# Normalising after the product in the second and third attention of a two-block layer stack

## What is computed

```python
# first block (called nsa): 4 groups x 4 heads, three softmaxes with gates
o = g[0] * o_cmp + g[1] * o_slc + g[2] * o_win
# second block, first layer (called ev): window over the tokens, plus context, plus a sink
p = jax.nn.softmax(jnp.concatenate([s_loc, s_ctx, s_sink], axis=-1), axis=-1)
o = jnp.einsum('bnkgqs,bnskd->bnqkgd', p[..., :nloc], vb) + jnp.einsum('bnkgqc,bckd->bnqkgd', p[..., nloc:nloc + lc], v_ctx)
# second block, second layer (called od): neighbourhood over the tokens, plus context
p = jax.nn.softmax(jnp.concatenate([s_loc, s_ctx], axis=-1), axis=-1)
```

## Time and profile before

| what | value |
|---|---|
| median of 3 runs | 2406.17 us (2405.99 to 2408.24) |
| the profiled execution | 2403.84 us |
| its span, first to last instruction | 2402.0 us |
| PE busy | 2318.0 us, 97% of the span |
| DVE, ACT, POOL busy | 1480.0, 921.2 and 249.1 us |
| mean granted TensorE clock | 0.982 of full speed |
| scores to last product of nsa | about 370 to 450 us of the span |
| the same of ev | about 1196 to 1263 us |
| the same of od | about 2130 to 2178 us |

### The profile page before, as it was taken

The page is one execution under the profiler, slowest core; times in us unless marked ns, Lnnn a source line. Parts: engine busy times, 40 slices in busy tenths (PEclk is TensorE's granted clock), DMA queues, the critical chain, the costliest instruction groups (busy, mean ns, idle before and its releaser), DMA issues.

```text
span 2402.0 us, 33724 instructions
## 1 busy us (share of the span) xinstructions
PE 2318.0 (97%) x14400; PEld 2015.2 (84%) x14400; DVE 1480.0 (62%) x1930; ACT 921.2 (38%) x1351; POOL 249.1 (10%) x235
## 2 busy tenths in 40 slices
PE   8999998889999999999989999999999999998999
PEld 7999895779998888888858888888888888878999
DVE  6584447577768776756765876424754333865544
ACT  6653336444454222224453322223422222544442
POOL 0030000101111101010010101100000101201110
PEclk9899998899999999999999999999999999999999
DMA  6444371255643544532202455222544322522553
GB/s 226 175 167 162 115 242 62 97 202 197 257 170 131 210 177 174 210 123 106 97 14 105 146 205 201 93 84 97 211 164 187 140 97 87 168 71 74 192 192 106
DMA packets 34834, 356.23 MB, mean 148 GB/s; under 512 B 3981, under 2 KB 6188, under 8 KB 8444
## 3 DMA queue, kind: packets, MB, share of 16 engines
q1 hardware_dynamic: 31788, 343.61, 38.6%
q0 software_dynamic: 2896, 10.46, 1.6%
HBM read 351.08 MB, written 1.13 MB: 147 GB/s over the span
## 4 chain that ended last, share of the span: by engine, by line
PE 89%; DVE 7%; ACT 3%; issue 1%; DMA 0%; POOL 0%; POOLq 0%; SPq 0%; DVEq 0%; ACTq 0%
PE psum L834 26%; PE psum L835 26%; PE psum L836 25%; PE psum L1126 2%; PE psum L882 1%; PE psum L883 1%; PE psum L884 1%; DVE ring_r L1825 1%; PE psum L1151 1%; DVE rr L1835 1%; PE psum L1121 1%; PE psum L1184 1%; PE psum L1095 1%; PE psum L1032 1%; PE psum L1023 1%
## 5 line engine op out<-in xcount | busy, mean ns | idle before, releaser
L834 PE MATMUL psum<-arena_r 128*128 128x256 f32 (+1 forms) x3384 | 1128.8, 334 | 20.5 <-DVE zT_r L1865 8.3
L836 PE MATMUL psum<-arena_r,ring_r 128*128 128x256 f32 (+1 forms) x3384 | 1119.3, 331 | 0.0
L835 PE MATMUL psum<-zT_r,arena_r 128*128 128x256 f32 (+1 forms) x2656 | 861.7, 324 | 0.0
L1351 ACT ACTIVATE arena_r<-ring 128x2048 fp32r<-128x2048 f32 (+1 forms) x252 | 473.5, 1880 | 705.8 <-PE psum L836 685.4
L834 PEld LDWEIGHTS psum<-arena_r 128*128 128x128 f32 x3384 | 637.2, 188 | 95.1 <-issue 21.8
L836 PEld LDWEIGHTS psum<-arena_r,ring_r 128*128 128x128 f32 x3384 | 639.3, 189 | 68.3
L1825 DVE TENSOR_TENSOR ring_r<-ring,arena_r 128x2048 fp32r<-128x2048 f32 (+1 forms) x252 | 568.3, 2257 | 195.5 <-ACT arena_r L1351 194.8
L835 PEld LDWEIGHTS psum<-zT_r,arena_r 128*128 128x128 f32 x2656 | 503.7, 190 | 45.1
L835 PE MATMUL psum<-arena_r 128*128 128x256 f32 (+1 forms) x1304 | 423.5, 325 | 0.0
L1976 DVE CUSTOM_DVE_ANT_0 psum<-arena,cb 128x1024 f32<-128x1024 f32 x256 | 318.1, 1302 | 0.0
L835 PEld LDWEIGHTS psum<-arena_r 128*128 128x128 f32 x1304 | 245.9, 189 | 20.4
(11 more groups left out here) (282 smaller groups left out, 1990.5 us busy)
## 6 DMA issues: line engine op xcount, KB each, us to landing
ring<-in_wf SPq DMA_DIRECT2D x75, 2048.0 KB, 7.9
ring<-in_w SPq DMA_DIRECT2D x41, 2048.0 KB, 7.9
arena<-in_w SPq DMA_DIRECT2D x72, 1024.0 KB, 9.8
ring<-in_wf SPq DMA_DIRECT2D x10, 1536.0 KB, 6.6
ring<-in_w SPq DMA_DIRECT2D x5, 1024.0 KB, 5.4
arena<-strip_scratch POOLq DMA_DIRECT2D x1, 2048.0 KB, 9.5
arena<-rpb_scratch POOLq DMA_DIRECT2D x16, 128.0 KB, 11.1
xT<-in_x SPq DMA_DIRECT2D x1, 1024.0 KB, 6.0
```

Of the source, the lines that this page charges most:

```text
L834: mm(b[c][:, at], whc, xh[:, k, at], start=(k == ks[0]), stop=False)
L835: mm(b[c][:, at], whc, xl[:, k, at], start=False, stop=False)
L836: last = mm(b[c][:, at], wlc, xh[:, k, at], start=False, stop=(k == ks[-1]))
L1351: A(W_hi[h % NHI][:, 0:n], ring[:, half_slot(h)], ACT.Identity).then_inc(sig("w_hi"), 1)
```

## The change

For ev and od, `turn` transposes the exponentials as they are, so that it no longer needs the diagonal matrices; it waits for all four exponentials of its unit instead. The diagonal matrices are still written by DVE (into two buffers in turn, the second one is `rr`), and a new step of PE, `spread_sums`, ahead of the last `multiply`, multiplies a block of ones by each of them: four matmuls of 128 rows by 64 by 128, which put the reciprocals of the sums on the rows and columns of the result's layout, in PSUM bank 4. ACT copies these 128 by 256 numbers to SBUF (into a half of `rt`) behind the last copy of the unit, and `att_done` multiplies the result by them in place of copying it. In DVE's loop `att_done(u-1)` now comes first, then `att_max(u+1, 1)`, then `att_norm(u)`, then `att_max(u+2, 0)`. For the first unit of an attention `att_max(u+1, 0)` and `att_max(u+1, 1)` come ahead of `att_norm(u)`. In nsa nothing changes.

```diff
--- before.py
+++ after.py
@@ -426,6 +426,14 @@
             at = (4 if g < 2 else 7) * BANK + (g % 2) * S
             return psum[:, at:at + S]
 
+        def att_sums(u):
+            return rt[:, S * (u % 2):S * (u % 2) + S]
+
+        def att_diag(u):
+            if u % 2:
+                return rr[:, :].rearrange("p (r t) -> p r t", r=4)
+            return E_diag if UNITS[u][0] == "ev" else O_diag
+
         def own(u, a, b):
             return small[:, 48 * (u % 2) + a:48 * (u % 2) + b]
 
@@ -1107,8 +1115,10 @@
                 def turn(i):
                     seg, blk = bs[i]
                     gb = gb0 + i
-                    if blk == bs[0][1]:
+                    if kind == "nsa" and blk == bs[0][1]:
                         pe.wait_ge(sig("att_p"), scaled_before(u) + seg + 1)
+                    if kind != "nsa" and i == 0:
+                        pe.wait_ge(sig("att_exp"), 4 * (u + 1))
                     if gb >= 2:
                         pe.wait_ge(sig("att_copied"), gb - 1)
                     pt = psum[:, (5 + gb % 2) * BANK:(6 + gb % 2) * BANK]
@@ -1117,13 +1127,8 @@
                             at = 2048 + (2 * (r % 2) + r // 2) * CMP_N if seg == 2 else place(seg, r) * S + blk * P
                         else:
                             at = r * BANK + blk * P
-                        if kind == "nsa":
-                            last = nc.tensor.transpose(pt[0:keys(i), r * P:(r + 1) * P], Pb[:, at:at + keys(i)],
-                                                       C("ident"))
-                        else:
-
-                            diag = (E_diag if kind == "ev" else O_diag)[:, r, :]
-                            last = mm(pt[:, r * P:(r + 1) * P], Pb[:, at:at + P], diag, start=True, stop=True)
+                        last = nc.tensor.transpose(pt[0:keys(i), r * P:(r + 1) * P], Pb[:, at:at + keys(i)],
+                                                   C("ident"))
                     last.then_inc(sig("att_turned"), 1)
 
                 def multiply(i):
@@ -1152,12 +1157,24 @@
                                       start=(i == 0), stop=(i == len(bs) - 1), skip_group_check=True)
                     last.then_inc(sig("att_mult"), 1)
 
+                def spread_sums():
+                    pe.wait_ge(sig("att_p"), scaled_before(u) + 1)
+                    diag = att_diag(u)
+                    for j in range(2):
+                        for a in range(2):
+                            at = 4 * BANK + j * P
+                            last = mm(psum[64 * a:64 * a + 64, at:at + P], C("ones")[:, 0:HD], diag[:, 2 * j + a, :],
+                                      start=True, stop=True)
+                    last.then_inc(sig("att_spread"), 1)
+
                 for i in range(len(bs)):
                     turn(i)
                     if i == min(2, len(bs) - 1):
                         between()
                     if i >= 1:
                         multiply(i - 1)
+                if kind != "nsa":
+                    spread_sums()
                 multiply(len(bs) - 1)
 
             def attention(u0, u1, Pb, PT, ready, beside=None, free_banks=None):
@@ -1675,6 +1692,9 @@
                         for part in range(4):
                             if parts_behind[part] == i and u + 1 < u1:
                                 att_exp(u + 1, Pb, part)
+                    if UNITS[u][0] != "nsa":
+                        act.wait_ge(sig("att_spread"), u - NSA_U[1] + 1)
+                        A(att_sums(u), psum[:, 4 * BANK:4 * BANK + S], ACT.Identity).then_inc(sig("att_spread_in"), 1)
 
 
             for i in range(2):
@@ -2371,14 +2391,8 @@
                 if kind == "ev":
                     link(v.tensor_tensor(out=sm[:, 0:4], in0=sm[:, 0:4], in1=own(u, 32, 36), op=ALU.add))
                 link(v.reciprocal(small[:, 36:40], sm[:, 0:4]))
-                first = (EV_U if kind == "ev" else OD_U)[0]
-                if u > first:
-                    dve.wait_ge(sig("att_turned"), batches_before(u))
-
-                v.tensor_tensor(out=E_diag if kind == "ev" else O_diag, in0=b3(C("ident"), 4, P),
+                v.tensor_tensor(out=att_diag(u), in0=b3(C("ident"), 4, P),
                                 in1=rep(small[:, 36:40], P), op=ALU.mult).then_inc(sig("att_p"), 1)
-                if u > first:
-                    att_done(u - 1, y)
 
             def att_done(u, y):
                 kind, g, t = UNITS[u]
@@ -2387,9 +2401,14 @@
                     k = 4 + 2 * g
                 else:
                     k = 2 * g
-                v.tensor_copy(y[:, k:k + 2, t * P:(t + 1) * P],
-                              psum[:, 7 * BANK:7 * BANK + 2 * P].rearrange("p (j t) -> p j t", j=2))\
-                    .then_inc(sig("att_out"), 1)
+                out, o = y[:, k:k + 2, t * P:(t + 1) * P], psum[:, 7 * BANK:7 * BANK + 2 * P]
+                o = o.rearrange("p (j t) -> p j t", j=2)
+                if kind == "nsa":
+                    v.tensor_copy(out, o).then_inc(sig("att_out"), 1)
+                else:
+                    dve.wait_ge(sig("att_spread_in"), u - NSA_U[1] + 1)
+                    v.tensor_tensor(out=out, in0=o, in1=att_sums(u).rearrange("p (j t) -> p j t", j=2), op=ALU.mult)\
+                        .then_inc(sig("att_out"), 1)
 
             def attention(u0, u1, Pb, y, beside=None, behind=None):
                 att_max(u0, (0, 1))
@@ -2398,11 +2417,17 @@
                 else:
                     att_max(u0 + 1, (0,))
                 for u in range(u0, u1):
-                    att_norm(u, Pb, y)
+                    kind = UNITS[u][0]
+                    if kind == "nsa":
+                        att_norm(u, Pb, y)
+                    elif u > u0:
+                        att_done(u - 1, y)
                     if u == u0 and beside is not None:
                         att_max(u0 + 1, (0,))
                     if u + 1 < u1:
                         att_max(u + 1, (1,))
+                    if kind != "nsa":
+                        att_norm(u, Pb, y)
                     if u + 2 < u1:
                         att_max(u + 2, (0,))
                     if behind is not None and u in behind:
```

## The result

The changed kernel takes 2389.34 us, median of 5 runs (2381.14 to 2395.61); the kernel before took 2405.99 beside it (median of 5). The ratio is 0.9927, interval 0.9912 to 0.9943: faster by 0.6 to 0.9%. Forecast were 2395.5 us and a range from 2389.5 to 2403.5. It does so by only 0.16 us, less than single runs differ; what stands clear of that is that the gain is larger than forecast. The profiled execution took 2390.42 us, 2388.6 of it span, beside 2403.84 and 2402.0 before.

The account below looks back on a forecast made before the run. PE was taken to bound the kernel, waiting in between for DVE and ACT. 7.9 us in ev and 5.8 in od, 13.7, less 3.0 for a clock fall, gave 10.7: 2395.5 us, range 2389.5 to 2403.5.

Parts of the forecast that it names:

- What bounds, and the direction: Whole kernel: PE leads but waits in between for DVE and ACT; sparing PE makes it faster, chance 0.78.
- 0.59 us for a turn: PE in ev and od: a turn by transposing takes 0.59 us in place of 1.09, 20.0 us spared over 40.
- the wait of 1.0 (1.12) for copy 0 in unit 12: Ev's unit 12: after two turns PE waits 1.0 us for ACT's copy 0; the unit takes 7.65 us.
- One fall in ev: Ev's unit 8, PE idle until 1210.4 after two short turns: the clock falls once where it did not before.
- the clock keeps falling, as in nsa: Rival, ev and od: clock at nsa's 0.81, 38% of 94 us at half clock; 2407 us, chance 0.16.
- DVE and ACT take a part back: Rival, 10 inner units: queues cost 0.5 us each, 5 us, hence 2400.5; chance 0.18, shared with half as many falls.
- The walk: Queues of ev and od followed with assumed durations: 7.9 us less in ev, 5.8 in od, together 13.7.
- Spreading at 0.60 for each unit, 7.2 in all: PE in ev and od: four added matmuls cost 0.60 us a unit, 7.2 for 12, perhaps less in four-batch units.
- The fall at 3.0 us: Price of ev's one clock fall: some 6 us at half clock do the work of 3, so 3.0 us lost.
- Unit 18's stall at 1.4 us: Od's unit 18, in the queue walk: PE stalls 1.4 us behind an exponential.
- Unit 12's 7.93 us: Ev before the change: unit 12 is bound by PE, its 7.93 us the sum of turns, products and scores, 7.94.
- the rival without a fall: Rival, ev: the clock does not fall, 13.7 us gained, up to 15 with shorter stalls; 2391 to 2392.5, chance 0.14.

## Why the prediction missed

The mechanisms were right and the sizes of three terms wrong, above all that of spreading. Right, by the steps of the prediction:

- *What bounds, and the direction.* PE led, and it gained. The number of records, 0.59 us for a turn (1243.77 to 1244.36 in the rows without spreading) and the wait of 1.0 (1.12) for copy 0 in unit 12 came as said, and no loss in the dense stages stands out of their spread.
- *The clock.* One fall in ev that had not been there, at the place forecast, gone without the idle time ahead of the first product (3.22 us), and no new one in od. The rival "the clock keeps falling, as in nsa" gave 2407 and is out: the batches of units 9 to 15 were turned by transposes at full clock, the fall came once with matmuls in place of transposes, and it went with the transposes kept. That ev had no fall before, with an idle 2.25 us at this place, was perhaps luck, since the kernel with identity matmuls fell behind 2.26. By the rule of the Trainium skill (TensorE: Matmul & The Clock Gate, PE-mode transpose) transposing doesn't count as PE being busy in the same way; in ev the traces show no effect of it where transposes stand among products and scores (granted clock 1.00 over 1200 to 1255.5 with the idle time filled). In unit 8, where two turns are the last work ahead of the idle time, the rule and the longer wait would both bring the fall, and the runs don't part them.
- *The part that would be late next.* "DVE and ACT take a part back" gave 2400.5 and is out: units 9 to 15 were all shorter than walked.

Wrong were the sizes, and all of them on one side. The walk with its fall comes to 102.6 us for the two stretches (113.3 - 13.7 + 3.0); 96.2 were measured. The 6.4 between them:

- *Spreading at 0.60 for each unit, 7.2 in all,* is the step that failed most; taken away, it gave back 1.9. It costs 0.44, and shortens its neighbours: the product ahead of it 0.48 in place of 0.58, the one behind it 0.53 in ev. That is 0.31 for each ev unit and 0.26 for each od unit, 8 x 0.31 + 4 x 0.26 = 3.5 us. The 0.60 was a real row, 8 records of the same form in four pairs; but that row stands between scores and a turn. Its pairs start 0.16, 0.11 and 0.11 us apart and the turn 0.22 behind the last, so 0.16 of the 0.60 are its unlike neighbours, while the spreading stands between two products of its own form and takes four steps of 0.11. The rest of the overcharge is the wait of 0.18 us for the last copy, which the prediction named ("so it may cost less") and then charged in full. And I put its lower bound nowhere: with an unknown charged twelve times, both ends belonged in the range.
- *The fall at 3.0 us.* It cost 1.8, by the throwaway matmuls in ev, and 1.76 in od. "Some 6 us at half clock do the work of 3" holds for a PE that has no waits in them; here a part of the slower work ran into time in which PE would have waited for DVE or ACT (od's 1.00 us wait; with the fall it is 0.42). 1.2 us.
- *Unit 18's stall at 1.4 us.* Measured some 0.6, from PE's timeline in od:

```profile
2156.77 0.66 PE L1146 MATMUL psum<-arena 128*64 128x128 f32 x8 [0.29 <-ACT arena L1674]
2157.25 0.61 PE L1166 MATMUL psum<-arena,cst 128*64 128x128 f32 x8
2157.92 0.67 PE L1146 MATMUL psum<-arena 128*64 128x128 f32 x8
```

  PE idles for 0.29 us (0.37 from start to start) ahead of the third product, and spreading lasts to the next start 0.67 us in place of 0.44, 0.23 of it a wait for the last copy. 0.8 us. On ACT the stall is longer: the exponential ahead of the late copy waits 0.98 us for its maximum, and PE has enough other work to see only the end of it:

```profile
2155.45 0.69 ACT L1663 ACTIVATE arena<-psum,small 128x512 f32<-128x512 f32 x1 [0.98 <-DVE small L2350]
2156.13 0.59 ACT L1674 ACTIVATE arena<-psum 128x512 f32<-128x512 f32 x1
```

- What is left, 0.9, I didn't isolate. The wait for the last copy, 0.18 us in a unit with four batches, may be a part of it: if the walk kept that wait beside the spreading that fills it, it counted the time twice. The walk isn't on record row by row.

One reading was right by luck. Unit 12's 7.93 us were called the sum of its parts with no wait in them, 7.94. But its first two turns, in one go, take 1.99 us and not 2.18, and the 0.18 us that this spares are the wait for the last copy, in the row of two products shown above.

These are attributions by unit, good to some tenths each; only the fall and the spreading were tried on their own. With the measured 17.1 in place of 10.7 the prediction's base gives 2406.17 - 17.1 = 2389.1. The range's low end, 2389.5, lies just below the rival without a fall, 2391 to 2392.5, which let the fall go and hardly moved the walk's other terms, spreading among them. (The prediction says that the range leaves out this rival's end; it doesn't.) But the fall did come, and the changed kernel was still faster than that rival: the missing microseconds were in the terms that it held.

## What to carry to other kernels

Read the cost of a group of matmuls from its start to the next start, and only from a row whose neighbours have the same form as those of the place that it will stand in. Look for a wait that the new work would fill before charging it in full. A clock fall costs less than half its length if it swallows waits: 1.8 us here for 6.8. And where an attention starts, look at what the first product waits for: two copies put ahead of two exponentials were worth 2.6 us, more than the order of DVE (1.8) and more than all of the spreading cost (1.9 at most).

## What the runs showed of the hardware that I had not expected

- A group of 8 records with 128 moving columns took 0.44 us with a 64 wide stationary operand, where they started in pairs 7 ns apart, and 1.09 with a 128 wide one, where each started alone; the product ahead of it was 0.10 us shorter in the first case. Moving columns and records are the same in both.
- The clock stood at half for 6.8 us in some traces and 3.4 in others, with the same program (ev in the changed kernel: 6.8 and 3.4); the difference was worth 0.3 us, which is within what the stretches repeat to.
- Idle time of PE of the same length, 2.25 and 2.26 us at the same place, was followed by a fall in one kernel and not in the other.
- Throwaway matmuls of 2.7 us, where PE stood idle, kept the clock at 2.4 GHz and made both attentions 1.8 us shorter: work that computes nothing had a negative price here, in a place where PE would have waited anyway.
